# The second block's odd mixer, taken by pairs of heads inside and behind weight slots

## The reference

```python
proj = h @ w_in_odd[i]
qc, kc, vc = split_cols(proj, [AX_Q, AX_KV, AX_KV])        # 1024, 256, 256
qc = rms_norm(qc.reshape(Bn, S, AX_HEADS, HEAD_DIM), ax_q_norm[i])   # 8 heads of 128
kc = rms_norm(kc.reshape(Bn, S, AX_KV_HEADS, HEAD_DIM), ax_k_norm[i])  # 2 heads
y = axial_attention(qc, kc, vc) @ w_out_odd[i]
x = x + y
# axial_attention: rope by grid row on the first half of a head, by grid column on the second, then
s = jnp.einsum('bqkgd,bjkd->bkgqj', qi, k) * scale
p = jax.nn.softmax(s, axis=-1)
o = jnp.einsum('bkgqj,bjkd->bqkgd', p, v)
```

## Time and profile before

| | us |
|---|---|
| median of three runs | 2765.02 |
| lowest, highest | 2763.86, 2766.34 |
| the profiled execution | 2765.99 |
| its span, first to last instruction | 2764.2 |
| TensorE busy in the span | 2650.8 (96%) |
| VectorE, ScalarE, GpSimd busy | 1186.9, 1099.7, 879.5 |

### The profile page before, as it was taken

One profiled execution on the slowest core, in us unless ns is written; L12 is line 12 of the kernel. 1 busy time (PEld: TensorE's weight loads), 2 busy tenths in 40 slices (PEclk: granted clock), 3 DMA queues, 4 the chain that ended last, 5 costly groups with the idle time before them and its releaser, 6 DMA issues. The chain is left out here.

```text
span 2764.2 us, 44695 instructions
## 1 busy us (share of the span) xinstructions
PE 2650.8 (96%) x17377; PEld 2352.3 (85%) x17377; DVE 1186.9 (43%) x1774; ACT 1099.7 (40%) x1517; POOL 879.5 (32%) x1092
## 2 busy tenths in 40 slices
PE   6999999999999999999999999889999999997999
PEld 3777788988888877787877889879999999995999
DVE  3222324226652222252222247654447565634644
ACT  2322333534334222243122247536664554443533
POOL 0222221320013222222222216214544455540554
PEclk8999999999999999999999999999999999997999
DMA  6343542330024344323344334234544345450454
GB/s 236 133 165 131 174 145 92 138 122 16 32 77 160 130 144 152 137 92 137 137 142 147 137 115 154 76 112 151 188 167 150 140 157 188 175 181 16 168 183 152
DMA packets 58503, 376.49 MB, mean 136 GB/s; under 512 B 6223, under 2 KB 12007, under 8 KB 14216
## 3 DMA queue, kind: packets, MB, share of 16 engines
q1 hardware_dynamic: 56988, 371.51, 37.5%
q10 hardware_dynamic: 1388, 3.16, 0.7%
HBM read 370.44 MB, written 3.16 MB: 135 GB/s over the span
## 5 line engine op out<-in xcount | busy, mean ns | idle before, releaser
L1648 POOL TENSOR_TENSOR WL<-RAW,WH 128x256 fp32r<-128x256 f32 x1088 | 879.2, 838 | 1872.3 <-ACT WH L1197 1872.3
L1197 ACT ACTIVATE WH<-RAW 128x1024 fp32r<-128x1024 f32 x544 | 545.7, 1050 | 958.4 <-PE PSA L549 940.7
L1671 DVE TENSOR_TENSOR WL<-RAW,WH 128x1024 fp32r<-128x1024 f32 x272 | 338.2, 1243 | 1139.5 <-ACT WH L1197 1139.4
L547 PE MATMUL PSA<-HH,WH 128*128 128x512 f32 (+1 forms) x1664 | 598.8, 360 | 16.8 <-DVE HL L1756 7.9
L548 PE MATMUL PSA<-HL,WH 128*128 128x512 f32 (+1 forms) x1664 | 589.5, 354 | 0.0
L549 PE MATMUL PSA<-HH,WL 128*128 128x512 f32 (+1 forms) x1664 | 588.7, 354 | 0.0
L547 PE MATMUL PSA<-GH,WH 128*128 128x256 f32 (+1 forms) x1664 | 529.4, 318 | 4.8 <-DVE GL L1689 4.8
L548 PE MATMUL PSA<-GL,WH 128*128 128x256 f32 (+1 forms) x1664 | 521.4, 313 | 0.0
L549 PE MATMUL PSA<-GH,WL 128*128 128x256 f32 (+1 forms) x1664 | 521.0, 313 | 0.0
L547 PEld LDWEIGHTS PSA<-HH,WH 128*128 128x128 f32 x1664 | 316.3, 190 | 75.8 <-issue 25.7
L549 PEld LDWEIGHTS PSA<-HH,WL 128*128 128x128 f32 x1664 | 316.4, 190 | 43.8
(11 more groups left out here) (298 smaller groups left out, 3064.1 us busy)
## 6 DMA issues: line engine op xcount, KB each, us to landing
RAW<-in_weights SPq DMA_DIRECT2D x272, 1024.0 KB, 4.8
ADA<-in_w_ada SPq DMA_DIRECT2D x65, 1024.0 KB, 4.8
Zada<-in_w_ada SPq DMA_DIRECT2D x7, 1024.0 KB, 13.4
scratch_bias<-BREL ACTq DMA_DIRECT2D x1, 2048.0 KB
SUMS<-in_c_sums SPq DMA_DIRECT2D x1, 1664.0 KB, 8.5
TB<-scratch_bias SPq DMA_DIRECT2D x1, 1536.0 KB, 10.8
X<-in_x SPq DMA_DIRECT2D x1, 1024.0 KB, 8.4
X<-in_ctx SPq DMA_DIRECT2D x1, 1024.0 KB, 12.4
```

Source lines behind the costliest of these rows:

```text
L547: pe.matmul(out, a_hi, b_hi, start=start, stop=False)
L1197: act.activation(WH[:, j, 4 * h:4 * h + 4, :], RAW[:, j, 4 * h:4 * h + 4, :], ACT.Copy)\
L1648: ins = pool.tensor_tensor(WL[:, j, kb, :], RAW[:, j, kb, :], WH[:, j, kb, :].bitcast(F32), ALU.subtract)
L1671: dve.tensor_tensor(WL[:, j, 0:4, :], RAW[:, j, 0:4, :], WH[:, j, 0:4, :].bitcast(F32), ALU.subtract)\
```

## The change

The separate mixer phase goes. The mixer is computed by pairs of heads p = 0 to 3, and each step of a pair is a piece that stands in a weight slot (after its fourth block, `inside_slot`) or behind one (`behind_pair_slot`). The slots count 0 to 5 for the input projection and 6 to 9 for the output projection. The input's columns come in another order: keys, query pairs 0 and 1, values, query pairs 2 and 3. The output projection takes its rows pair by pair: slot 6 + p holds the 256 rows of pair p and all 1024 output columns, and is multiplied as soon as that pair's output is there. Its results for all four column units so gather in banks 0 to 3 over four slots. A product with a matrix of zeros opens each of these banks and another one closes it. The residual, the next input's parts and the sums of squares all come in and behind slot 9. The heads' norm gains are put into the tables of the rope (`angles`, four operations and a memset on VectorE before the input projection) with a second, turned copy of the gains among the parameters. Key and query factors: the key's is put on after the rope, the query's as before in the exponentials' scale.

```diff
@@ plan_slots
-        if l:
-            plan.append(dict(kind="odd", slot=slot, unit=unit))
         phase("down", 8 if l == 0 else 4, 4, tokens=256, kin=8, gate=None, layer=l, per=2 if l == 0 else 1, first=True,
-              by_half=(l == 0))
+              by_half=(l == 0), by_pair=(l == 1))
@@ token_major: the values' slot is now the fourth
-            return 2 if ph["kind"] == "in_odd" and i == 5 else 0
+            return 2 if ph["kind"] == "in_odd" and i == 3 else 0
@@ TensorE, weights_phase, body: pieces in the middle of a slot and behind it
+                        if kind == "in_odd":
+                            def each(kb, i=2 * it + j):
+                                if i % 2 == 0:
+                                    h_block(kb)
+                                if kb == 4:
+                                    inside_slot(ph, i)
...
+                            if ph["late"]["fed_by"].get("by_pair"):
+                                unit_sums(ph["late"]["fed_by"], 2)
                             unit_sums(ph["late"]["fed_by"], 3)
...
+                        if kind == "in_odd":
+                            behind_pair_slot(ph, jj)
@@ TensorE, the output projection
+                def units_by_pair():
+                    ready = n.at(gl_ready) - 4
+                    any_rows = H2H[:, 0:2, :].rearrange("p a t -> p (a t)")
+                    for c in (0, 2, 3, 1):
+                        pe.wait_ge(bank_read[c // 2], ph["unit"] + BANK_CREDIT)
+                        if c == 1:
+                            pe.wait_ge(key_read, 3)
+                        pe.matmul(bank(c), ZERO[:], any_rows, start=True, stop=False)
+                    def part(p, r, c):
+                        for m in range(2):
+                            w = slice(P * m, P * m + P)
+                            mm = three(bank(c)[:, NL * m:NL * m + NL], WH[:, p % 2, 4 * r + c, w], WL[:, p % 2, 4 * r + c, w],
+                                       G2H[:, 2 * p + r, :], G2L[:, 2 * p + r, :], False, False)
+                        return mm
+                    for p in range(4):
+                        slot = ph["slot"] + p
+                        slot_half(slot, 0)
+                        pe.wait_ge(gl_ready, ready + p + 1)
+                        if p < 3:
+                            for c in range(4):
+                                part(p, 0, c)
+                            slot_half(slot, 4)
+                            inside_slot(ph, 6 + p)
+                            for c in range(4):
+                                mm = part(p, 1, c)
+                            mm.then_inc(mm_done, 1)
+                            behind_pair_slot(ph, 6 + p)
+                        else:
+                            slot_half(slot, 4)
+                            for c in range(4):
+                                part(p, 0, c)
+                                part(p, 1, c)
+                                mm = pe.matmul(bank(c), ZERO[:], G2H[:, 0:2, :].rearrange("p a t -> p (a t)"), start=False, stop=True)
...
+                                if c > 1:
+                                    unit_sums(ph, c - 2)
@@ TensorE, the pieces (pair_turn, pair_scores, pair_transposes, pair_output, pair_sums replace attention)
+            def inside_slot(ph, i):
...
+                if i == 2:
+                    column_sums(bank(6))
+                    pair_turn(slice(0, 2))
+                if 5 <= i <= 8:
+                    pair_output(i - 5)
+                if i in (5, 6):
+                    evicted(i - 1)
+                    pair_turn(slice(2 * (i - 1), 2 * i))
+            def behind_pair_slot(ph, i):
+                base = n.at(gl_ready) if ph["kind"] == "in_odd" else n.at(gl_ready) - 4
+                if i == 6:
+                    pe.wait_ge(turned_read, 5)
+                    pair_sums(3)
+                    pair_scores(3)
+                    pair_transposes(2, base)
+                    return
+                if i == 5:
+                    pair_sums(2)
+                if 4 <= i <= 7:
+                    pair_transposes(i - 4, base)
+                if 3 <= i <= 5:
+                    pair_scores(i - 3)
+                if i in (2, 3):
+                    pe.wait_ge(turned_read, i - 1)
+                    pe.wait_ge(key_read, i - 1)
+                    pair_sums(i - 2)
+                    pair_turn(slice(2 * (i - 1), 2 * i))
@@ ScalarE, behind_pair_slot (behind the split for slot i + 2)
+                if i == 1:
+                    squared(0)
+                    squared(1)
+                    root(KRMS[:])
+                elif i == 2:
+                    squared(2)
+                    query_root(0)
+                elif i == 3:
+                    exps(0)
+                    query_root(1)
+                elif i == 4:
+                    weights_turned(0)
+                    squared(4)
+                    exps(1)
+                    output_high(0)
+                elif i == 5:
+                    squared(5)
+                    query_root(2)
+                    weights_turned(1)
+                    exps(2)
+                    output_high(1)
...
@@ VectorE, behind_pair_slot
+                if i == 1:
+                    link(rope(slice(0, 2), 1))
+                    n.take(sq_used)
+                    dve.tensor_scalar(KRMS[:], bank(6), 1.0 / P, EPS, ALU.mult, ALU.add).then_inc(dve_to_act, 1)
+                    dve.engine_nop().then_inc(key_read, 1)
+                elif i == 2:
+                    n.take(act_to_dve)
+                    link(dve.reciprocal(KRMS[:], KRMS[:]))
+                    k = Z2[:, 0:2, :].rearrange("p a t -> p (a t)")
+                    dve.tensor_tensor(k, k, KRMS[:], ALU.mult).then_inc(key_ready, 1)
+                    query_mean(0).then_inc(dve_to_act, 1)
+                    dve.engine_nop().then_inc(key_read, 1)
+                    query_rope(0)
+                    query_factor(0)
+                elif i == 3:
+                    maxima(0)
+                    query_mean(1).then_inc(dve_to_act, 1)
+                    query_rope(1)
+                    query_factor(1)
+                    softened(0)
+                elif i == 4:
+                    maxima(1)
+                    query_rope(2)
+                    softened(1)
+                    output_low(0)
...
+                elif i == 6:
+                    query_mean(3).then_inc(dve_to_act, 1)
+                    dve.engine_nop().then_inc(key_ready, 1)
+                    query_factor(3)
+                    maxima(3)
+                    softened(3)
+                    output_low(2)
+                elif i == 7:
+                    output_low(3)
@@ host: order of the weight stream
-            stream += whole(a["w_in_odd_2"][0]) + whole(a["w_out_odd_2"][0])
+            stream += slots(a["w_in_odd_2"][0], [1024, 0, 256, 1280, 512, 768])
+            for p in range(4):
+                part = a["w_out_odd_2"][0][256 * p:256 * p + 256]
+                stream.append(part.reshape(2, P, 4, 256).transpose(1, 0, 2, 3).reshape(1, P, SLOT))
```

More of the change, by code:

```diff
@@ new lines, in pair_turn, with pair_scores @@
+            def pair_turn(blocks):
+                pe.matmul(bank(7), rot_ax, Z2[:, blocks, :], start=True, stop=True).then_inc(turned_ready, 1)
+            def pair_scores(p):
+                if p == 0:
+                    pe.wait_ge(key_ready, 2)
+                else:
+                    n.take(score_read)
+                n.take(rope_ready)
+                q = 2 * (1, 2, 4, 5)[p]
+                for h in range(2):
+                    for b in range(2):
+                        mm = pe.matmul(bank(4 + h)[:, NL * b:NL * b + NL], Z2[:, q + h, P * b:P * b + P], Z2[:, p // 2, :],
+                                       start=True, stop=True)
+                mm.then_inc(window_scored, 1)
@@ L1123, in attention, with pair_transposes @@
+            def pair_transposes(p, base):
+                n.take(soft_ready)
+                if p == 0:
+                    pe.wait_ge(rope_ready, n.at(rope_ready) + 1)
+                else:
+                    pe.wait_ge(gl_ready, base + p)
+                for h in range(2):
+                    if h:
+                        pe.wait_ge(turned_read, min(p, 2) + 3)
+                        if p == 2:
+                            pe.wait_ge(key_ready, 3)
                     for jb in range(2):
@@ L1136, in attention, with pair_sums @@
-                n.skip(gl_ready, 4)
+                        mm = pe.matmul(bank(6)[:, NL * h:NL * h + NL], Z2[:, 6 + jb, P * (p // 2):P * (p // 2) + P],
+                                       PTO[:, 2 * p + h, NL * jb:NL * jb + NL], start=(jb == 0), stop=(jb == 1))
+                mm.then_inc(o_ready, 1)
+            def pair_sums(p):
+                n.take(sq_ready)
+                buf = S2[:, n.squares % 2, :]
+                n.squares += 1
+                b, at = ((6, 0), (6, 8), (1, 256), (7, 0))[p]
```

(4 more changed lines are left out.)

265 lines of the change are left out of this document (154 added, 111 removed).

## The result

| | before | changed |
|---|---|---|
| median, us | 2765.68 (4 runs) | 2733.47 (4 runs) |
| lowest, highest | 2763.86, 2771.93 | 2730.32, 2737.96 |
| ratio | | 0.9883, 95% interval 0.9871 to 0.9894 |

The account below looks back on a forecast made before the run. TensorE's weight-slot stream bounds the kernel, except 63.8 us in the odd mixer. Less 27.7 mixer, 1.8 zero products and 2.2 waits, 32.1 us off gives 2733.9, forecast 2733.0 us against the median; range 2729.5 to 2742.

Parts of the forecast that it names:

- The hole: Second block's odd mixer, between input and output projection: 63.8 us in which no weight slot is worked on.
- mixer and zero products: TensorE's remaining mixer work, 27.7 us, plus 8 added products with the zero matrix, 1.8 us.
- The waits: TensorE waits 1.5 us behind slot 3 before the first scores, 0.7 us behind slot 5 before pair transposes; sum 2.2 us.
- the walk: Engine queues followed slot by slot with trace durations to find TensorE's remaining waits: sum 2.2 us, range 0 to 8.
- The thin margin at slot 8: Lower half of slot 8's weight split on VectorE ready at +8.2 us from slot 7's start, TensorE there at +8.6.
- Table loads: Six more on ScalarE, 1.28 us each, hidden where it waits anyway; without that cover 7.7 us.
- A: Rival: VectorE pieces slower beside GpSimd, 0.56 us per operation; waits 8 to 17 us, 2739 to 2748 us; chance 0.12.
- B: Rival: ScalarE table switches cost 2.66 us each, exponentials late behind slots 4 and 7: 2738 us; chance 0.04.
- C: Rival: late mixer pieces delay weight splits and following slots, exposing 13 us a pair: 2783 us; chance 0.03.
- D: Rival: a wait on a counter holds the pieces together behind slot 5; waits near 34 us, 2765 us; chance 0.03.

Follow-up runs that it names:

- e1: Changed kernel with three orders on VectorE altered, same work: 2733.1 us, ratio 0.9875 to the kernel before; norm-mean interval 89.82 us against 91.94.
- e4: Changed kernel with VectorE's maxima of each pair computed four times over: 2742.91 us (one run).
- e12: Changed kernel with VectorE's maxima of each pair computed eight times over: 2762.56 us (one run).
- e2: Changed kernel without the roots of the query factors of pairs 1 to 3, so six ScalarE table loads fewer: 2735.73 us (one run).
- e3: Changed kernel with two more ScalarE table loads, forced by tiny activations, ahead of each pair's exponentials: 2735.24 us (one run).
- e11: Changed kernel with six more GpSimd operations behind each of its weight splits for eight slots, beside VectorE's ropes and softenings: 2738.26 us (one run).
- e5: Changed kernel with all pair pieces put together between input and output projection, on three engines: 2770.5 us, ratio 1.0011 to the kernel before.
- e8: Kernel before the change, plus 64 unread products of 512 columns issued where TensorE waits in the mixer: ratio 0.9987 to the kernel before.
- e6: Changed kernel with only the pieces of slots 2 to 5 put together behind slot 5: 2759.5 us, ratio 0.9975 to the kernel before.
- e7: Changed kernel with only the pieces of slots 6 to 8 put together ahead of slot 6: 2748.36 us (one run).

## Why the prediction was right

- **The hole and what stays of it.** The interval without the hole is 125.73 - 63.8 = 61.93 us; what the changed kernel has above that is 30.0: 1.7 of waits and 28.3 of mixer and zero products, where I had 29.5. The term is mis-sized by 1.2 us (by 1.6 against e1, which has no waits: 89.82 - 61.93 = 27.9). I took a piece's price from the busy time of its group, whose last instruction's end overlaps what follows. The starts in the changed kernel (TensorE's timeline) give the price in a full queue:

```profile
2497.05 1.89 PE L1194 MATMUL PSA<-PTO,Z 128*128 128x256 f32 x8
2498.78 1.02 PE L1155 MATMUL PSA<-Z,SMALL 128*128 128x512 f32 x2
2499.24 0.68 PE L549 MATMUL PSA<-H2H,WH 128*128 128x256 f32 x1
2499.76 0.28 PE L550 MATMUL PSA<-H2L,WH 128*128 128x256 f32 x1
```

  Outputs of a pair 1.73 us (priced 1.8). The rotation ends where L549's slot would start at its step of 0.12: 2499.76 - 0.12 - 2498.78 = 0.86 (priced 0.95). Behind query sums it is 0.94, so the six products of 512 columns make only 0.3 us of the 1.2, and the four outputs another 0.3. Query sums start 0.81 us ahead of what follows them in two places (2484.08 to 2484.89, 2516.05 to 2516.86; priced 0.93). The rest was not followed up.
- **The closeness is luck.** The terms give an interval of 125.73 - 32.1 = 93.6 us; it measured 91.94, so they are 1.7 us out, 1.2 by the pieces and 0.5 by the waits. The medians of the whole times differ by 32.2 us where the intervals differ by 33.8, and this 1.6 us of spread hides it. The mechanism and its size to 1.7 us are shown, agreement to 0.5 us is not.
- **The waits.** 1.03 and 0.70 against 1.5 and 0.7; e1 shows that both came from VectorE's order, as the walk had it.
- **The thin margin at slot 8.** VectorE's timeline and TensorE's, the changed kernel:

```profile
2526.33 1.21 DVE L1820 TENSOR_TENSOR WL<-RAW,WH 128x1024 fp32r<-128x1024 f32 x1
```
```profile
2527.02 1.04 PE L1185 MATMUL PSA<-SMALL,SBO 128*128 128x128 f32 x8
2527.82 0.36 PE L549 MATMUL PSA<-GH,WH 128*128 128x256 f32 x1
```

  The half is written at 2527.54, TensorE wants it at 2527.82: 0.3 us, forecast 0.4. e4 and e12 show that lateness there starts no convoy.
- **Table loads.** 1.28 us each and hidden: e2, e3.
- **Rivals.** A: the mechanism is real, but no rope or softening met it here (e11). B: false (e2, e3). C: lateness is not handed on (e4, e12). D: the pieces do stand in the slots. What D would have cost is e5, 2770.5 us, 5 more than I wrote.
- **What the sum hid.** By subtraction from 63.8 us the clock never had to be priced. Of the 33.8 us 21.3 were idle time (23.1 to 1.8) and 12.5 busy time (102.64 to 90.14, with 8 more instructions); e8, which won back 10.1 us by the clock alone, shows what most of the 12.5 are.

## What to carry to other kernels

When a chain of narrow handovers stands alone between dense streams, cut it into pieces that are one handover long and put each behind a slot of the stream; the gain is the idle time and also the clock that goes with it (21.3 and 12.5 us here). Walk the in-order queues with durations from the trace: here the walk's idle time was 0.5 us too high for the change, 2.1 where 35 us of work was added, and 3.7 where whole pieces were moved (e5, e6; 1.1 in e7); take prices from the distance of starts, not from a group's busy time. Judge such a change by a stretch between two marks that both kernels have, which repeated to 0.01 us where whole runs spread by 8, and look on the other engines for an order that hands over first what TensorE asks for first.

## What the runs showed of the hardware

- The same score or output instructions take 7.2 us at clock 1.00 and 8.9 us in the sparse mixer; eight outputs take 1.99 and 3.78 us in e7 at 1.00 and 0.50. Of e5's 37.1 us above the changed kernel 14.4 are busy time, the larger part of it by the clock.
- A wait of 3.53 us left the clock at 1.00, one of 3.06 us in the same run did not (e4), and in e7 it stood at 0.50 from 2512 to 2514 with no wait over 1.1 us before.
- Products issued only to keep TensorE busy can run at the lower clock themselves (14 of 512 columns in 5.04 us, 34 in 8.32 us later on) and delay what stands behind them, in e8 by 4.1 and 1.9 us.
- VectorE's operation with two SBUF inputs of 512 columns takes 0.69 us, and up to 1.1 beside GpSimd; with one input from PSUM it keeps its 0.69 (e11).
- Three switches of ScalarE's tables in a row, each with a small activation, start 1.50 us apart: 1.28 of load, 0.21 of activation (e3).
